# Hybrid encoder step: the reciprocal set ahead of query splits, sample ends in two steps, and seven smaller moves of the written order

## The reference

```python
z = rmsnorm(x) @ w_in        # q | k | v | forget logits | pooling input u | memory query qm | 3 gates
o_fox  = softmax(q k^T / 8 + c_q - c_k, causal) v      # 8 heads x 64; samples also see 512 cached rows
o_pool = (trailing means over 2, 4, 8, 16 tokens - u) @ w_pool * s_pool
o_mem  = softmax(qm mk^T / sqrt(128)) mv               # 4 heads x 128, 256 memory rows
h = x + (sum_b sigmoid(gate_b) * (o_b @ w_br_b)) @ w_out
y = rmsnorm(h + relu(rmsnorm(h) @ w_up)**2 @ w_down)
```

## Time and profile before

| what | value |
|---|---|
| runs of the kernel | 1939.59, 1940.26, 1940.54 us (median 1940.26) |
| the profiled execution's own time | 1939.99 us |
| its span, first to last instruction | 1938.3 us |
| TensorE matmuls, busy | 1900.1 us (98%) |
| TensorE weight loads, busy | 1865.1 us (96%) |
| VectorE | 1223.0 us (63%) |
| ScalarE | 843.7 us (44%) |
| GpSimd | 516.3 us (27%) |

### The profile page before, as it was taken

How to read it: one execution, slowest core, us unless ns; L and a number is a source line. 1 busy time by engine, 2 the same in 40 slices (tenths; PEclk the granted TensorE clock), 3 DMA queues, 4 the chain that set the end, 5 groups by cost and what they waited for, 6 DMA issues and landing times. The chain is left out here.

```text
span 1938.3 us, 32954 instructions
## 1 busy us (share of the span) xinstructions
PE 1900.1 (98%) x12587; PEld 1865.1 (96%) x12587; DVE 1223.0 (63%) x2285; ACT 843.7 (44%) x1671; POOL 516.3 (27%) x547
## 2 busy tenths in 40 slices
PE   7999999999999999999999999999999999999998
PEld 7999999999999999999999999999999999999997
DVE  6675545454557665554333467687787877777765
ACT  6444435353546543442223332344444544444445
POOL 1003324150612122000000003276554333333320
PEclk9999999999999999999999999999999999999999
DMA  6451311312266633453232322233433433333323
GB/s 188 121 133 50 93 47 49 99 35 86 62 228 203 205 114 101 151 165 110 84 89 84 93 83 76 85 107 88 124 88 88 124 88 88 91 89 88 88 93 98
DMA packets 243601, 202.40 MB, mean 104 GB/s; under 512 B 16750, under 2 KB 217966, under 8 KB 243317
## 3 DMA queue, kind: packets, MB, share of 16 engines
q1 hardware_dynamic: 243445, 200.29, 34.2%
HBM read 166.62 MB, written 33.64 MB: 103 GB/s over the span
## 5 line engine op out<-in xcount | busy, mean ns | idle before, releaser
L1616 PE MATMUL ps<-act_hi,w_hi 128*128 128x384 f32 x1128 | 386.7, 343 | 1.2 <-DVE fox_q_lo L2646 0.9
L1616 PE MATMUL ps<-act_hi,w_lo 128*128 128x384 f32 x1128 | 377.9, 335 | 0.0
L1616 PE MATMUL ps<-act_lo,w_hi 128*128 128x384 f32 x1128 | 377.5, 335 | 0.0
L581 DVE TENSOR_TENSOR w_lo<-w_raw,w_hi 128x512 fp32r<-128x512 f32 (+1 forms) x200 | 197.6, 988 | 124.1 <-ACT w_hi L563 123.3
L1600 PE MATMUL ps<-ffs_hi,w_hi 128*128 128x288 f32 x832 | 245.6, 295 | 2.2 <-DVE h L2579 2.2
L1600 PE MATMUL ps<-ffs_hi,w_lo 128*128 128x288 f32 x832 | 245.3, 295 | 0.0
L1600 PE MATMUL ps<-ffs_lo,w_hi 128*128 128x288 f32 x832 | 244.9, 294 | 0.0
L1585 PE MATMUL ps<-bp_hi,pw_hi 128*128 128x288 f32 x784 | 231.5, 295 | 0.2 <-DVE pw_lo L2534 0.2
L1585 PE MATMUL ps<-bp_lo,pw_hi 128*128 128x288 f32 x784 | 231.3, 295 | 0.0
L1585 PE MATMUL ps<-bp_hi,pw_lo 128*128 128x288 f32 x784 | 231.2, 295 | 0.0
L563 ACT ACTIVATE w_hi<-w_raw 128x512 fp32r<-128x512 f32 (+1 forms) x200 | 152.7, 763 | 161.1 <-PE ps L1600 119.3
(11 more groups left out here) (352 smaller groups left out, 4181.4 us busy)
## 6 DMA issues: line engine op xcount, KB each, us to landing
w_raw<-in_w_down_dram SPq DMA_DIRECT2D x112, 256.0 KB, 3.2
pair_raw<-in_w_up_dram SPq DMA_DIRECT2D x28, 1024.0 KB, 5.4
w_raw<-in_w_in_dram SPq DMA_DIRECT2D x44, 512.0 KB, 4.2
merged<-prod SPq DMA_DIRECT2D x48, 192.0 KB, 2.0
prev<-merged SPq DMA_DIRECT2D x48, 192.0 KB, 4.1
foxs_vraw<-in_cache_fox_v_dram SPq DMA_DIRECT2D x8, 1024.0 KB, 6.1
foxs_kraw<-in_cache_fox_k_dram SPq DMA_DIRECT2D x7, 1024.0 KB, 5.4
x_in<-in_x_prompt_dram SPq DMA_DIRECT2D x8, 512.0 KB, 4.5
```

The costliest lines, as they stand in the source:

```text
L581: nc.vector.tensor_tensor(W[c % 2][1][:, 0:kt, :], w_raw[c % 2][:, 0:kt, :], W[c % 2][0][:, 0:kt, :].bitcast(F32), ALU.subtract).then_inc( ...
L1616: last = nc.tensor.matmul(bank(b)[:, 0:width], W[k][a][:, t, :], moving[z][:, t, j * width:(j + 1) * width], start=(t == 0 and n == 0), st ...
```

## The change

Nine moves; no product, transpose, split or transfer is added or taken away, but one ACT instruction on one column (with the function Exp) is added.

1. In `mem`, where queries of a further head are split, DVE takes the reciprocal of the same entry ahead of that split instead of at the start of the next entry (three places).
2. The end of the first set of samples: values of the last sample ahead of half 4 of the first gate of the second branch (before: ahead of half 3), the turn of the output and its readers ahead of half 5. The entry of the last turn is number 25, behind `mem_parts`.
3. The same for the second set of samples: values stay, the turn goes one half later.
4. The wait of PE for the last sample output goes from block 0 to block 2 of the first branch tile that needs it.
5. In `first`, DVE splits the first two key tiles ahead of the clears instead of behind them (both sets).
6. Pool entry 3 goes from half 0 to half 1 of q of pair 0.
7. After the high part of pool entry 3 ACT takes one Exp of one column, so the table for Exp is loaded there.
8. At the first seam the two additions of down tile 0 come ahead of the preparation of weights and of squares.
9. The same at the middle seam, ahead of the preparation of parts.

```diff
     for g in range(BT):
-        put(("u", g + 1, 0, 0) if g + 1 < BT else ("q", 0, 0, 0), "pool", g)
+        put(("u", g + 1, 0, 0) if g + 1 < BT else ("q", 0, 0, 1), "pool", g)
...
-        put(where[3 + s], "sample", 0, s)
+        put(where[3 + s + s // (3 * NB)], "sample", 0, s)
     put(where[28], "mem_parts", 0)
+    put(where[29], "sample", 0, 3 * NB + 1)
...
+    put(where[7 + BT * QT + 5 + 3 * NB], "sample", 1, 3 * NB + 1)
...
+        def next_queries(s):
+            return s % QT == 2 and s // QT + 1 < MH
...
-                    if i == NB:
-                        turned_out()
+                elif part == 1 and i == NB:
+                    turned_out()
...
-                            if s.i == 1:
+                            if s.i == 1 and j == 2:
                                 pe.wait_ge(sa["o_done"], NB)
...
                 nc.scalar.activation(X[0][:, g, :], pooled[:], ACT.Copy).then_inc(po["d_hi"], 1)
+                if g == BT - 1:
+                    nc.scalar.activation(small[:, 18:19], eps_t[:], ACT.Exp)
...
-                elif part == 0:
+                elif part == 1 and i == NB:
                     out_low()
                     out_high()
...
-                if 1 <= s <= M_UNITS:
+                if 1 <= s <= M_UNITS and not next_queries(s - 1):
                     reciprocal(u - 1)
...
-                if s % QT == 2 and s // QT + 1 < MH:
+                if next_queries(s):
+                    reciprocal(u)
                     queries_lo(s // QT + 1)
...
                     dve.wait_ge(at_s["pv_over"], PAIRS + M_PAIRS * k)
+                    keys_lo(a, 0, 0)
...
-                keys_lo(a, 0, part)
-                if part == 1:
+                else:
+                    keys_lo(a, 0, 1)
...
-                if part == 0 and i == NB:
+                if part == 1 and i == NB:
                     out_sum()
...
+                early = kind == "down" and i == 0 and s in (0, SEAM // 2 - 2)
+                if early:
+                    down_add(s, i)
                 for job in prepared(n):
                     prep_lo(*job)
...
                 if kind == "down":
-                    down_add(s, i)
+                    if not early:
+                        down_add(s, i)
```

## The result

| kernel | median us | lowest to highest | runs |
|---|---|---|---|
| before | 1940.68 | 1939.59 to 1941.80 | 11 |
| with the nine moves | 1944.41 | 1943.45 to 1946.00 | 11 |

The change costs 3.7 us: ratio 1.0021, 95% interval 1.0013 to 1.0028. The prediction was 1940.0, between 1936.0 and 1942.7; the time is outside, on the slow side. The medians differ by 0.19%, at the edge of what the prediction counted as no change, but the interval of the ratio leaves no room for none. The profiled execution of the changed kernel took 1945.89 us, its span is 1944.2 us, 5.9 more than before's.

What follows compares the result with a forecast made beforehand. PE, busy 98% of the span, was taken as the bound, so only its stops could be won. Terms: 5.65 won, 5.4 lost; 1939.99 becomes 1939.75, plus 0.27 for the median: 1940.0 us, range 1936.0 to 1942.7.

Steps and rivals of the forecast that it cites:

- Moves 6 and 7: At q and k of pair 0: one PE idle of some 4.9 us replaces two short ones; 3.2 us lost, bounds 2.9 to 4.6.
- The clock: Rival: PE's clock falls to 1.2 GHz during the new stop at k, 1.6 us lost, 1941.6 in all; chance 0.25.
- The rival in which the clock stays low: Behind k the low clock lasts, every us costing 0.5; with 10 us 1944.9; chance 0.05.
- The bounds of the costs: Low and high values given for the terms; around the forecast they were said to give 1937.9 to 1943.
- The table load without drain: Exp table load ahead of q costs 1.28 us, not 2.66 with a drain, by which the sum would be 1.4 worse.
- The table at its old place: Pair 0's first turn no longer has the 1.28 us table load in its chain: 0.7 us won, bounds 0 and 0.9.
- Keys ahead of clears: Move 5, first low parts of keys: PE's 0.6 stop goes, POOL's copies limit sample 0's scores; 0.3 us won, bounds 0, 0.75.
- First end of samples: Moves 2 and 4: two PE waits go, but the first memory turn comes later; 2.2 us lost, bounds 1.7 and 2.7.
- Reciprocals: Move 1, three memory turns: PE's stops for POOL's division shrink; 3.3 us won, bounds 2.4 and 3.7.
- Second end: Move 3, second set of samples: PE's wait of 0.8 is covered by half a gate; 0.95 us won, bounds 0.5 and 1.
- Seams: Moves 8 and 9, PE's stops for additions: 0.4 us won at the first seam, 0 at the middle one.
- the two that would have made it wrong: ACT starting on q before 128, or the first memory turn, counted from qm's last read-out before the samples' end, no later.

Runs made afterwards that it cites:

- experiment 4: The kernel before with moves 6 and 7, the 2.1 MB store issued behind the load of k's weights: 1945.06 us, 4.9 over before.
- experiment 5: The changed kernel with 36 spare matmuls on PE ahead of the first block of k: 1942.24 us, 1.9 over before.
- experiment 10: The kernel before with moves 1 and 3, and move 7's Exp put ahead of ACT's wait for the last means: 1935.32 us, 5.0 below before.
- experiment 2: The changed kernel with moves 6 and 7 undone, all the others kept: 1937.60 us, 2.6 below before.
- experiment 12: Experiment 10 with only PE's turn of pool entry 3 one half later, other engines' parts at their old place: 1935.47 us, 0.15 from experiment 10.
- experiment 8: The kernel before with moves 2 and 4 alone: 1942.47 us, 2.1 over before.
- experiment 9: Experiment 8 with the last sample output's turn and readers still later, behind the weights of the second branch's first tile: 1945.74 us, 5.4 over before.

## Why the prediction was wrong

**Moves 6 and 7, forecast 3.2 lost: 5.7 (6.1 with the early lateness), and 2.1 more for the clock.** The step that failed is "the split of the weights of k, 1.05 us, now goes there and ends at 117.65". It took ACT's idle for the only condition and did not ask when the raw weights land. They came at 119.50, 2.4 us after ACT was free, because their load was queued behind 2112 KB; experiment 4 removed that and gave nearly the forecast stop, 5.19 for 4.9. The rest of the step held: the order on DVE, the sums, the table load, all with their durations. (Its terms add up to 129.35, not 129.45, and the 0.2 taken off for overlaps was 0.07.)

**The clock, forecast 0.25: it fell.** Every profile with the late turn and no spare matmuls shows it, six of six, also that with nearly the stop of the forecast (experiment 4). The argument "the idle is only a little longer than the one after which the clock fell" spoke for the fall, and was read as speaking against it. Its price was right: forecast 1.6 with 3.3 us at half rate; 1.5 in experiment 4 with 3.2 us, 2.1 in the first trace with 4.6 us, 1.9 by experiment 5. The half rate at the start is read from the count of matmuls alone, since the row's own clock column shows 1.00 there. The rival in which the clock stays low did not come: it was 1.00 again after 3.1 to 5.5 us of PE's work in all six. The page "TensorE: Matmul & The Clock Gate" of the Trainium skill (Why this matters for your kernels) warns of such gaps between bursts; by that rule, the traces agree.

With the 2.4 us for the landing alone the sum would have given 1942.4, with the fall alone 1941.6, both inside the range; only the two together, 1944.0, lie outside. The one rival that was priced with the fall left k's start where it was forecast; with k 2.9 later, as in the first trace, the same sum gives 1944.5. That this is near the measured median is luck in part, since the trace itself lost 5.9 and other terms were off as well. The bounds of the costs, all taken at their bad ends, add up to 1944.7, not to the 1943 that the text gives.

**The table load without drain: right.** It takes 1.28 us at its new place, from 130.99, with the next instruction at 132.28. The page "ScalarE: Activation LUTs" of the Trainium skill (What ACT_TABLE_LOAD costs) would have had 2.66; neither this trace nor that of experiment 10 shows the drain.

**The table at its old place, forecast 0.7 won: 0.8.**

**Keys ahead of clears, forecast 0.3 won: 0.1.** What came last wasn't POOL's copies. The clears now stand between the keys and the queries' low part, on which the same scores wait:

```profile
560.83 0.59 DVE L2409 MEMSET foxs_qpad_hi<- 128x640 f32 x1
...
562.64 0.27 DVE L2412 MEMSET foxs_pt<- 128x256 f32 x1
```

A stop of 0.6 went and one of 1.0 came.

**First end of samples, forecast 2.2 lost: 2.9 in the first trace, 2.2 to 2.9 over six.** The mechanism was right. The readers' 1.9 us were exact. The parts started 1.2 late in the first trace instead of 0.5 (8.2 at a shift of 7.0): the values ended 0.9 later, about as said, but the load of `mqs_raw` took 4.2 us to land, not 3.4. This isn't an error of the assumption alone. The load took 3.9 in the trace of before, 3.4 in experiment 2 and in the second profile of the changed kernel, where the end cost the forecast 2.2, 3.6 in experiment 5 (2.3), and 4.1 to 4.2 in the three others, where it cost 2.8 or 2.9. The forecast took one value where the landing varies by 0.7 us between executions of one program; its reason, a queue with more time to empty, is not shown.

**Reciprocals, forecast 3.3 won: 3.3**, with the late division at the third split as said (0.4). **Second end, 0.95 won: 1.0.**

**Seams, forecast 0.4 won: 0.3 lost in the first trace.** At the first, 0.9 was won where PE had stopped, and 0.8 lost again by 1297.6, around two short stops that are new, for `w_lo` (0.13) and for an addition (0.10): the little slack of the blocks behind was worth nothing, and 0.1 is left of the 0.4. At the middle seam the forecast stop for `w_lo` came, 1.13 us. In this trace ACT's split came 5.9 after its time of before, at a shift of 5.5, having waited 1.38 for its transfer instead of 1.08, and the next addition made PE stop 0.6 instead of 0.2. That is not shown to be a cost of move 9. In the five traces with the move, the shift over this seam changed by -0.6 to +0.4 (the wait for the transfer was 0.24 to 1.39), and in the eight traces without it by -0.5 to +0.5 (0.47 to 1.57). The forecast of 0 for it stands within that.

```profile
1543.03 0.63 ACT L565 ACTIVATE w_hi<-w_raw 128x512 fp32r<-128x512 f32 x1 [1.38 <-DMA w_raw<-in_w_down_dram]
```

Together: the forecast was 0.25 won against before; in the trace it is 5.9 lost. Of the difference of 6.1, moves 6 and 7 make 2.5, the early lateness 0.4, the clock 2.1, the first end 0.7, the seams 0.7 and the keys 0.2, less some 0.4 that the table's old place and the samples' middle gave more than said. The 2.5 and a fall of the clock are found in all four traces with moves 6 and 7 whose weights queued behind the store. The early lateness, the 0.7 of the first end and the 0.4 of the middle seam are not found in all. That the medians differ by only 3.7 stays open.

The signs named in the prediction came nearly all (a stop for `mqs_lo`, one of 1.0 at the first memory turn, one for `w_lo` at the middle seam, four waits gone), and neither of the two that would have made it wrong did. What told of the miss was the size of the stop at q, 7.4 for 4 to 5, and the clock.

## What to carry to other kernels

An idle stretch of an engine is room for a moved instruction only if its inputs are there; a transfer that lands late with nobody waiting is in no list of waits and must be looked up by its tile. A stop of PE is worth its size only if what PE waits for next comes earlier too: two stops on one chain are one (experiment 12), and a stop won ahead of a chain that doesn't end earlier is a longer wait later (experiment 8). A new stop of several us has to be priced together with the clock behind it. Terms of a few tenths of a us that hang on when a transfer lands need more than one trace: the same load took 3.4 and 4.2 us in two executions of one program.

## What the runs showed of the hardware

The granted clock fell during PE's stops at q in all six profiles in which PE was idle there for 5.2 to 7.4 us, but not at the same point of the stop: in three executions of the same program it fell at 134.5, and twice at about 131.6, with PE idle from 129.4 on in the first and from 128.9 on in the two others. For `mqs_lo` PE stopped for 2.2 to 2.9 us in six profiles; the clock fell within 0.1 us of the stop's end in experiment 2 (2.2) and experiment 8 (2.8) and stayed at 1.00 in the three profiles of the changed kernel (2.9, 2.2, 2.8) and in experiment 5 (2.4). In experiment 9 (5.4) it fell. The fall cost 1.4 to 2.5 us at q, where PE's own work was the bound, with 3.1 to 5.5 us of that work at 0.50. In experiments 2 and 8 it cost nothing that shows, as the other engines' chain was the bound there: 7.19 us from the first memory scores to the first turn, with and without it.

A load of 512 KB issued behind a store of 2112 KB on the same queue landed after 11.2 to 11.8 us in the thirteen traces with this order; issued ahead of it, after 5.4 (experiment 4).
